# Gram products that alternate heads in four PSUM banks, values centred before the scan, and dense filler moved within the pair

## The reference

```
sa = einsum('bhij,bhj->bhi', S, a_t)
S  = S * w_t + sa[..., None] * b_t + v_t[..., None] * k_t
y  = einsum('bhij,bhj->bhi', S, r_t)
...
y = y_f + y_b
mean = jnp.mean(y, axis=-1, keepdims=True)
var = jnp.mean(jnp.square(y - mean), axis=-1, keepdims=True)
y = (y - mean) * lax.rsqrt(var + GN_EPS)
y = y * ln_x_gain + ln_x_bias
bonus = sum(r * k_bonus * r_k_h) * v
out = (y + bonus) * g
```

## Time and profile before

| | |
|---|---|
| median of 3 executions | 2285.89 us (2285.77 to 2287.3) |
| the profiled execution | 2286.4 us, its span 2284.6 us |
| PE busy | 2122.5 us, 93% of the span |
| PE weight loads, beside it | 1914.8 us |
| DVE, ACT, POOL busy | 1315.9, 921.7 and 356.5 us |
| mean granted PE clock | 0.965 |

### The profile page before, as it was taken

One profiled execution on the slowest core, in us unless ns is written; L12 is line 12 of the kernel. 1 busy time (PEld: TensorE's weight loads), 2 busy tenths in 40 slices (PEclk: granted clock), 3 DMA queues, 4 the chain that ended last, 5 costly groups with the idle time before them and its releaser, 6 DMA issues.

```text
span 2284.6 us, 39096 instructions
## 1 busy us (share of the span) xinstructions
PE 2122.5 (93%) x14475; PEld 1914.8 (84%) x14475; DVE 1315.9 (58%) x2119; ACT 921.7 (40%) x1544; POOL 356.5 (16%) x424
## 2 busy tenths in 40 slices
PE   6999997999999999999999887879999999999996
PEld 6999996988888888888888776778988979889794
DVE  4666465566667666666766634454545555454454
ACT  4555332444434444444444323343434334334342
POOL 0000001333333333333333320000000000000000
PEclk9999998999999999999999868989999999999998
DMA  6546654322222232223221304535565655556552
GB/s 194 148 130 165 180 140 129 81 69 71 79 79 68 72 79 79 64 70 79 71 69 49 111 1 147 166 111 178 179 176 179 175 180 184 167 182 183 170 180 91
DMA packets 415085, 281.25 MB, mean 123 GB/s; under 512 B 14042, under 2 KB 372668, under 8 KB 414012
## 3 DMA queue, kind: packets, MB, share of 16 engines
q1 hardware_dynamic: 414620, 277.43, 42.0%
q10 hardware_dynamic: 416, 3.15, 0.3%
HBM read 278.46 MB, written 2.10 MB: 123 GB/s over the span
## 4 chain that ended last, share of the span: by engine, by line
issue 51%; PE 35%; DVE 6%; POOL 4%; ACT 2%; DMA 0%; SPq 0%; POOLq 0%; DVEq 0%; ACTq 0%
PE bank L1378 6%; PE bank L1379 5%; PE bank L1380 5%; PE bank L1583 3%; PE bank L1633 2%; PE bank L1648 2%; PE bank L1394 1%; PE bank L1395 1%; PE bank L1396 1%; PE bank L1653 1%; POOL st L1302 1%; POOL CT L1324 1%; DVE wlo L770 1%; PE bank L1754 1%; PE bank L1450 1%
## 5 line engine op out<-in xcount | busy, mean ns | idle before, releaser
L1378 PE MATMUL bank<-xT,whi 128*128 128x256 f32 x2784 | 822.1, 295 | 13.2 <-PE bank L1396 5.1
L770 DVE TENSOR_TENSOR wlo<-raw,whi 128x2048 fp32r<-128x2048 f32 (+1 forms) x286 | 533.0, 1864 | 492.2 <-ACT whi L424 431.3
L1379 PE MATMUL bank<-xT,whi 128*128 128x256 f32 x2784 | 788.3, 283 | 0.0
L1380 PE MATMUL bank<-xT,wlo 128*128 128x256 f32 x2784 | 787.8, 283 | 0.0
L1378 PEld LDWEIGHTS bank<-xT,whi 128*128 128x128 f32 x2784 | 534.6, 192 | 23.2 <-issue 18.4
L1379 PEld LDWEIGHTS bank<-xT,whi 128*128 128x128 f32 x2784 | 535.1, 192 | 1.2
L1380 PEld LDWEIGHTS bank<-xT,wlo 128*128 128x128 f32 x2784 | 533.3, 192 | 0.0
L424 ACT ACTIVATE whi<-raw 128x2048 fp32r<-128x2048 f32 x166 | 316.9, 1909 | 287.9 <-PE bank L1396 287.9
L1394 PE MATMUL bank<-whi,ft 128*128 128x512 f32 x512 | 205.3, 401 | 12.3 <-PE bank L1396 9.3
L1395 PE MATMUL bank<-wlo,ft 128*128 128x512 f32 x512 | 202.2, 395 | 0.0
L1396 PE MATMUL bank<-whi,ft 128*128 128x512 f32 x512 | 202.1, 395 | 0.0
(11 more groups left out here) (214 smaller groups left out, 3092.7 us busy)
## 6 DMA issues: line engine op xcount, KB each, us to landing
raw<-in_w_in SPq DMA_DIRECT2D x106, 1024.0 KB, 6.0
raw<-in_w_ffn_up SPq DMA_DIRECT2D x64, 1024.0 KB, 6.3
raw<-in_w_ffn_down SPq DMA_DIRECT2D x64, 1024.0 KB, 5.0
raw<-in_w_out SPq DMA_DIRECT2D x16, 1024.0 KB, 5.0
raw<-in_w_in SPq DMA_DIRECT2D x4, 768.0 KB, 4.6
xtok<-in_x SPq DMA_DIRECT2D x2, 1024.0 KB, 5.9
upg<-in_g_up SPq DMA_DIRECT2D x16, 128.0 KB, 3.4
hres<-in_x ACTq DMA_DIRECT2D x1, 2048.0 KB, 8.9
```

What stands on the lines that cost most here:

```text
L770: x = V.tensor_tensor(wlo[:, u_static % 2, part], raw[:, u_static % 4, part], whi[:, u_static % 2, part].bitcast(f32), ALU.subtract)
L1378: M(bank[:, 0:T], h, xT[:, k, 0, :], start=k == 0, stop=False)
L1379: M(bank[:, 0:T], h, xT[:, k, 1, :], start=False, stop=False)
L1380: x = M(bank[:, 0:T], l, xT[:, k, 0, :], start=False, stop=k == KT - 1)
```

## The change

- The constant `ones_mean` (1/64 in each head's block) becomes `centred`, the identity less it. The transposes of the values become products with `centred`, into the upper half of bank 2. The mean product, `centre` and their semaphores go. ACT squares y straight from bank 2 and copies it behind that; `scale` reads ysb.
- `gram(m)` becomes `heads(g)`: four groups instead of eight products, each with both heads of one token block and direction, in the order bh head 0, bh head 1, kh head 0, kh head 1, in banks 3 and 4 (forward) and 5 and 6 (backward). `gate` and `bonus` go to bank 2, the transposes of the first level to banks 4 and 3.
- The y products of one direction alternate heads: V V U U instead of V U V U per head.
- PE order in the tail: group 0, values, y products, group 1, variance, 3 slices of the next filler unit, gate, group 2, bonus, group 3, broadcast, 3 slices. `EARLY = 6` slices are so done before the pair begins, and of the 9 at its head 3 are left, behind the first transposes.
- DVE: neighbours behind level 4, differences behind level 5, shift behind the levels; the decay scans in scan step 0, `inverse(0)` before `modified`, `inverse(1)` and `hats(0)` in step 1, `hats(1)` behind it; both halves of the cut of unit 2 ahead of the masks; masks 6 and 7 ahead of the bonus and the merge.
- Prologue on PE: unit 0 of pair 1 goes before `squares`, unit 1 before `values`.

```
@@ constants @@
-    c[:, C_MEAN:C_MEAN + P] = same / 64.0
+    c[:, C_CENT:C_CENT + P] = np.eye(P) - same / 64.0
@@ ACT pair @@
                 w("lg")
-                A.activation(gup[:], PB[4][:, 0:T], ACT.Copy)...
+                w("bonv")
+                A.activation(gup[:], PB[2][:, 0:T], ACT.Copy)...
...
                 w("ym")
+                A.activation(ysq[:], PB[2][:, 0:T], ACT.Square)...
                 A.activation(ysb[:], PB[2][:, 0:T], ACT.Copy)...
                 if n is not None:
                     values(n)
-                w("ycs")
-                A.activation(ysq[:], yc[:], ACT.Square)...
@@ DVE keep @@
+                    bank = PB[3 + 2 * d + h]
+                    if m == 0:
+                        dve.wait_ge(s["ym"].sem, s["ym"].before(self.n))
-                    self.w("gram", m + 1)
+                    self.w("gram", m // 2 + 1)
@@ DVE pair, levels @@
+                        if nx and l == 4 and d == 0:
+                            nx.neighbours()
+                        if nx and l == 5 and d == 0:
+                            nx.differences()
+                if nx:
+                    nx.shift()
@@ DVE pair, tail @@
+                nx.hats(1)
                 cut_pair(0, d2, 0)
-                nx.hats(1)
+                cut_pair(0, d2, 1)
                 gram.keep(0)
-                tail.centre()
                 gram.keep(1)
                 tail.variance()
                 gram.keep(2)
+                gram.keep(3)
                 gram.lasts()
                 tail.spread()
-                gram.keep(3)
-                cut_pair(0, d2, 1)
                 gram.keep(4)
+                gram.keep(5)
                 tail.scale()
-                gram.keep(5)
+                gram.keep(6)
+                gram.keep(7)
                 tail.add_bonus()
                 gram.bonus()
                 tail.gate()
-                gram.keep(6)
                 tail.merge()
-                gram.keep(7)
@@ PE heads @@
+                    ts = slice(P * tb, P * tb + P)
                     for a, src in enumerate((bh[d], kh[d])):
+                        for h in range(2):
+                            hp = slice(64 * h, 64 * h + 64)
+                            x = M(PB[3 + 2 * d + h][:, T * a:T * a + T], src[hp, ts], AR[d][hp, :, ts], ...)
@@ PE pair, head @@
-                filler(3)
                 for d in range(2):
                     w("dt0", d + 1)
+                    w("gmask", 6)
...
                     inc(x, "d0p")
-                    filler(4 if d == 0 else 2)
+                    if d == 0:
+                        filler(3)
@@ PE pair, tail @@
                 if gram:
+                    gram.heads(0)
                     gram.values()
...
                 inc(x, "ym")
                 if gram:
-                    gram.gate()
-                    gram.gram(0)
+                    gram.heads(1)
                     nx.w("nkk")
-                w("ye")
-                x = M(PB[7][:, 0:T], ones_mean, ysb[:], start=True, stop=True)
...
                 inc(x, "var")
                 if gram:
+                    dense(2, d2, 0, EARLY // 2)
+                    gram.gate()
+                    gram.heads(2)
                     gram.bonus()
+                    gram.heads(3)
                 w("vrep")
...
                 inc(x, "vbc")
+                dense(2, d2, EARLY // 2, EARLY)
@@ PE prologue @@
             p0.lora_a()
+            dense(0, 1)
             p0.squares()
             p0.norms()
+            dense(1, 1)
             g0 = Gram(0)
...
+            dense(2, 1, 0, EARLY)
```

More of the change, by code:

```diff
@@ L621, in pair @@
                 w("lg")
-                A.activation(gup[:], PB[4][:, 0:T], ACT.Copy).then_inc(s["gups"].sem, 1)
+                w("bonv")
+                A.activation(gup[:], PB[2][:, 0:T], ACT.Copy).then_inc(s["gups"].sem, 1)
                 A.activation(gt[:], raw4[:, 3, 1:T + 1], ACT.Tanh, scale=0.5).then_inc(s["gate_t"].sem, 1)
@@ L1049, in keep @@
                     inc(V.copy_predicated(G[:, :, 1 - d, 2 * tb + h, :].rearrange("p (a b) c -> p a b c", a=2), mask,
[L1050 removed]
+                                          bank[:, :].rearrange("p (a b c) -> p a b c", a=2, b=2)), "gmask")
                 def lasts(self):
@@ L1130, in pair @@
                             cut_pair(2, d1, l - 4)
+                        if nx and l == 4 and d == 0:
[4 more added lines that the diff above has]
+                    nx.shift()
                 for c in range(2):
-                    if nx and c == 0:
-                        nx.neighbours()
-                    elif nx:
-                        nx.inverse(0)
+                    if nx and c == 1:
+                        nx.inverse(1)
                     w("ue", c + 1)
@@ L1141, in pair @@
                     if nx and c == 0:
-                        nx.shift()
+                        nx.products(0)
+                        nx.products(1)
                     elif nx:
-                        nx.inverse(1)
+                        nx.hats(0)
                     w("dum", c + 1)
@@ L1159, in pair @@
                         if nx:
-                            nx.products(0)
-                            nx.products(1)
+                            nx.inverse(0)
                             nx.modified()
-                if nx:
-                    nx.hats(0)
                 tail = Tail(i)
                 if nx is None:
-                    tail.centre()
                     tail.variance()
@@ L1551, in values, with heads @@
                 def values(self):
-                    pe.wait_ge(s["due"].sem, s["due"].before(self.n))
                     self.w("shifted")
+                    self.w("tws")
                     for tb in range(2):
-                        x = nc.tensor.transpose(PB[5][:, P * tb:P * tb + P], sh[:, 2, P * tb:P * tb + P], ident)
+                        x = M(PB[2][:, T + P * tb:T + P * tb + P], sh[:, 2, P * tb:P * tb + P], centred, start=True, stop=True)
                     inc(x, "vtp")
                 def gate(self):
-                    pe.wait_ge(s["rese"].sem, s["rese"].before(self.n))
+                    self.w("vts")
                     for q in range(2):
-                        x = M(PB[4][:, 0:T], upg[:, q, :], gact[:, q, :], start=q == 0, stop=q == 1)
+                        x = M(PB[2][:, 0:T], upg[:, q, :], gact[:, q, :], start=q == 0, stop=q == 1)
                     inc(x, "lg")
-                def gram(self, m):
+                def heads(self, g):
                     w = self.w
-                    tb, d, h = m // 4, m // 2 % 2, m % 2
-                    if tb == 0 and h == 0:
+                    tb, d = g // 2, g % 2
+                    if tb == 0:
                         w("khs", d + 1)
@@ L1588, in bonus @@
                     self.w("t2")
-                    pe.wait_ge(s["sme"].sem, s["sme"].before(self.n))
-                    x = M(PB[6][:, 0:T], ones_half, rk[:], start=True, stop=True)
+                    self.w("vts")
+                    x = M(PB[2][:, T:2 * T], ones_half, rk[:], start=True, stop=True)
                     inc(x, "bonm")
@@ L1749, in pair @@
                     M(PB[2][:, ts], Sm[:, d2nd, :], AS[:, d2nd, 1, :], start=True, stop=False, skip_group_check=True)
-                    for h in range(2):
-                        hp, q = slice(64 * h, 64 * h + 64), 2 * tb + h
-                        for d in range(2):
-                            c = tb if d == 0 else 1 - tb
+                    for d in range(2):
+                        c = tb if d == 0 else 1 - tb
+                        for h in range(2):
+                            hp, q = slice(64 * h, 64 * h + 64), 2 * tb + h
                             M(PB[2][hp, ts], Vt[:, tb, hp], gram_of(d, q, 3), start=False, stop=False, skip_group_check=True)
+                        for h in range(2):
+                            hp, q = slice(64 * h, 64 * h + 64), 2 * tb + h
                             x = M(PB[2][hp, ts], U[:, c, 2 * d + h, :], gram_of(d, q, 1), start=False, stop=d == 1, skip_group_check=True)
@@ L1778, in pair @@
                 inc(x, "vbc")
-                if gram:
-                    for m in range(5, 8):
-                        gram.gram(m)
+                dense(2, d2, EARLY // 2, EARLY)
             for j in range(4):
@@ L1789, in _ @@
             p0.lora_a()
+            dense(0, 1)
             p0.squares()
             p0.norms()
+            dense(1, 1)
             g0 = Gram(0)
             g0.values()
+            g0.heads(0)
+            g0.heads(1)
             g0.gate()
-            for m in range(8):
-                g0.gram(m)
-                if m == 3:
-                    g0.bonus()
-            for j in range(2):
-                dense(j, 1)
+            g0.bonus()
+            g0.heads(2)
+            g0.heads(3)
+            dense(2, 1, 0, EARLY)
             with pe.Fori(0, PAIRS - 2, 1) as i:
```

81 lines of the change are left out of this document (33 added, 48 removed).

## The result

The kernel before takes 2286.99 us (median of 5), the changed one 2296.97 us (5 executions, 2292.01 to 2301.92): ratio 1.0047, 95% interval 1.0036 to 1.0058. Forecast were 2265 us and a range of 2240 to 2280. The profiled execution of the changed kernel took 2292.01 us, with a span of 2290.2 and a mean granted clock of 0.945 (before 0.965).

A forecast was written before the change was run, and what follows sets the result against it. TensorE's instruction stream was taken to set the pace, beside a DVE and ScalarE chain nearly as long. Loop -17, clock +18, prologue -16 and end -6 against 2286.4 gave 2265 us, range 2240 to 2280.

The forecast's parts named there:

- The overlap of heads: TensorE's Gram groups: two heads side by side take 1.1 us a group, 3.1 us saved per pair.
- merge, gup, W: Queue from DVE's merge through ScalarE to W becomes the late one; 1.4 of TensorE's 4.5 us saved per pair arrive.
- Neighbours and differences: DVE's neighbours' sum and difference go into gaps before level updates, hidden but for 0.1; 0.2 us a pair taken.
- The prologue: Before the loop: two dense units move into TensorE's waits, first transposes at about 399.2 instead of 415.4 us, -16.2.
- the clock behind the hole: TensorE's idle stretch before a pair's first W level product halves the clock in nearly every pair: 1.4 us each, +20.
- DVE's copy of the norm: In the scan stage: moved shift and scans use time in which DVE waited; no cost for this copy.
- broadcast to first W level product: TensorE from the variance's broadcast through the transposes: 4.83 and 4.86 us become 1.7 and 6.7 a turn.
- y to broadcast: TensorE from the first V product of y to the variance's broadcast: 10.79 us becomes 9.2 a turn.
- The end: Last transition -3.5 us; last pair: copy, mean and subtraction leave the chain, y products shrink; together -6.
- Rival 2: The clock stays at 2.4 GHz in the hole, -18 more: 2247 us; 27%.
- rivals 3 and 4: 3: program order rules, groups 0.25 us longer, 2275 us, 10%. 4: alternating heads don't overlap, about 2302 us, 7%.
- rival 5: TensorE's saving arrives whole, 14 x 4.5 us, with prologue and end: 2201 us; 4%.

The follow-up runs named there:

- e1_warm: Changed kernel with six throw-away fp32 products per pair, three behind the second transposes and three ahead of the first W level product: 2262.29 us.
- e5_ar: Changed kernel with one more wait on POOL, AR's first products waiting for DVE's copy of the norm: 2280.42 us.
- e2_norm: Changed kernel with both decay scans on DVE moved behind the norm of the keys: 2320.54 us.
- e11_merge: Changed kernel with mask 7 on DVE moved behind the merge: 2274.78 us.
- e3_order: Changed kernel with each group's products in the old order, both of head 0, then both of head 1, in the four banks: 2293.2 us.
- e8_cut: Changed kernel with the second half of ScalarE's cut of unit 3 moved behind the first W: 2314.62 us.
- e12_fill: Changed kernel with TensorE's tail recast alone: no early slices, variance broadcast ahead of the last group, nine slices between the two sets of transposes: 2279.51 us.
- e14_half: Changed kernel with three throw-away products per pair behind the second transposes, the wait for W left empty: 2285.97 us.
- e7_cast: Changed kernel with TensorE's tail recast (broadcast ahead of the last group, nine slices between the transposes) and mask 7 behind the merge: 2248.47 us.
- e10_cast_ar: Changed kernel with the recast tail, mask 7 behind the merge and POOL's AR waiting for the norm's copy: 2241.62 us.
- e13_real: Kernel with recast tail, late mask 7 and AR's wait, plus two filler slices moved ahead of the first W level product: 2213.02 us.

## Why the prediction was wrong

**Right.** The overlap of heads, to a few hundredths (1.07 for 1.1; y stretches 1.02 for 1.0). That the late one would no longer be TensorE's stream but merge, gup, W, with an idle TensorE before the second transposes (0.57) and before the first W level product; I had put 3.1 us idle into this place, it is 4.0 on average. That the clock would fall in nearly every pair. Neighbours and differences between the levels: levels 16.83 against 16.66 at full clock, +0.17 for 0.2. The prologue: -15.8 for -16.2.

**The terms of the sum that failed**, in the loop:

| term | forecast, us | measured, us | shown by |
|---|---|---|---|
| the clock behind the hole | +20 | +31 | e1_warm |
| DVE's copy of the norm | 0 | +13 | e5_ar, e2_norm |
| broadcast to first W level product | -18 | -5 | e11_merge for most |
| y to broadcast | -22 | -27 | the trace alone |
| norm to y: group 0, values, second residual | +18 | +12 | the trace alone |

Both columns are 14 times the differences in the table of stretches, but for the clock, which has its own run; neighbours and differences, +3 and +2, complete the sums, +1 and +27 (before rounding).

1. **The clock.** I priced a spell by the one fall of the kernel before, 3.4 us long, at 1.4 us. The mechanism and its place were right, the size off: the spells last 6.8 us or more and each costs 2.4. The upper bound, twice 1.4, would have held it; I did not carry that bound into the range, which ended 15 us above the forecast.
2. **A missed neighbour.** "Shift and scans use time in which DVE waited": true for DVE. But the scans release POOL's products, which waited for them before, and these fell on the one short copy that TensorE stands behind. I had asked what the moved step delays, and not what it sets free.
3. **Gate and merge.** I saw that DT would be ready sooner ("The masks end at 775.7 now") and counted it as a gain. That it would run beside gate and merge and stretch these by 0.8 us I did not price, although in the trace of before the first DT of that pair takes 1.95 us, begun beside a cut on DVE, where the second takes 1.16:

```profile
773.13 1.21 DVE L770 TENSOR_TENSOR wlo<-raw,whi 128x1024 fp32r<-128x1024 f32 x1
```
```profile
773.40 1.95 POOL L1331 TENSOR_TENSOR DT<-G,lmk 128x512 fp32r<-128x512 f32 x1 [1.21 <-DVE G L1049]
```

4. **The end**, -1.8 for -6. The second transposes of the last pair still wait for DT, longer than in the earlier trace rows:

```profile
1331.71 1.10 PE L1618 MATMUL bank<-cst,DT 128*128 128x128 f32 x4 [2.61 <-POOL DT L1334]
```

The last transition gained 1.5 us and not 3.5; y to broadcast gained 1.5 and not 2.6; and the stage behind took 1.0 longer. There the clock was still at 0.50 for 4.9 us instead of 3.7, which may be the reason; it wasn't tried.

No rival had this outcome. Rival 2 fell with the first spell, rivals 3 and 4 fell with e3_order and the group's 1.07 us, rival 5 with the wait for W. The slower side came from three small costs beside each other, 11, 13 and 13 us, each in a place that the rows named but whose neighbour on POOL I had not looked at. Two stretches came out 11 us better together than forecast; 6 of them are the stall at the second residual, 0.33 instead of 0.77 us a turn.

Of the two rules that I weighed, both from the Trainium skill, page "TensorE: Matmul & The Clock Gate", strict program order (Part 3) is contradicted more clearly than by the earlier trace rows: in e3_order a product starts ahead of one of the other row half that was issued before it. Half rate as the default that activity releases (Part 1) agrees with e1_warm, which holds 1.00 by work that has no use. It leaves open the one fall in the loop of the kernel before, which came behind a stretch with TensorE busy for 5.28 of 5.30 us, and why e8_cut and e12_fill fared worse than e14_half with the same idle time.

**Open.** Why DVE and POOL stretch each other on some pairs of steps (the copy 0.36 to 1.30, the gate 0.41 to 0.92) and not on others was not tried. The traces show a pattern, though. The step that starts second is the one that is stretched: the copy starts 0.06 us behind AR and the gate 0.59 behind DT, but in e2_norm the cut starts 0.16 us ahead of AR, and there AR takes 1.58 us instead of 0.67:

```profile
753.37 1.20 DVE L772 TENSOR_TENSOR wlo<-raw,whi 128x1024 fp32r<-128x1024 f32 x1
```
```profile
753.53 1.58 POOL L1311 TENSOR_TENSOR AR<-sh,Pd 128x256 f32<-128x256 f32 x1 [0.36 <-DVE Pd L1002]
```

And a DVE step that takes one operand from a PSUM bank keeps its time: `bon<-bank,sh` starts 0.25 us behind DT and takes 0.42 us, while the gate behind it, with both operands in SBUF, takes 0.92. The value of the four banks by themselves in a whole turn was not tried either.

## What to carry to other kernels

When a change shortens TensorE's stream below a chain of the other engines, price the hole twice: once as idle time and once as the clock that falls behind it. Here 4.0 us idle in a turn of 62.5 cost another 2.4 in levels at half rate (2.2 as a mean of all 14 turns), and two slices of real work moved into the wait ahead of the late step were worth 22 to 29 us. For each step that moves earlier, look up who waits for its semaphore and what that engine will then run beside.

## What the runs showed of the hardware

- Products of 64 rows in different row halves overlap without regard to program order: bh and kh of one head issued before the other's still ran as bh, bh, kh, kh, two heads in 1.07 us, each with a free output bank.
- 96 throw-away products of 256 columns made a kernel 35 us faster (2296.97 to 2262.29); in its loop the granted clock stayed at 1.00 and a turn took 60.35 us instead of 62.53.
- A DVE copy of 128x128 (two of them in 0.36 us) took 1.30 us while POOL multiplied 128x256 tiles; a DVE multiplication of 128x256 went from 0.41 to 0.92 us beside POOL's DT. Where DVE had started first it was POOL's multiplication that grew, from 0.67 to 1.58 us, and a DVE step with one operand in PSUM kept its 0.42 us.
- The clock fell more often with more idle time in the hole, but not by that time alone. Of the 13 turns behind the first it fell in all with 4.0 us idle (changed kernel), in 11 with 2.9 us (e14_half), in four (e7_cast) and seven (e10_cast_ar) with 2.0 us, and in none with 1.6 us (e1_warm) or 1.2 us (e13_real). Against the order, it fell in all 13 with 2.9 us (e12_fill) and with 2.8 us (e8_cut).
